# A hybrid attention, retention and mixture-of-experts block: new order and finer pieces at its head, its first refills and its tail

## The reference

```python
h = rms_norm(x, norm1_gain)
proj = h @ w_in          # attention q, k, v; indexer q, k, w; retention q, k, v, gate
out_a = dsa_attention(...)   # 64 of 256 keys chosen by the indexer, 8 heads
out_b = silu(g_b) * group_norm(retention(rotary(q_b), rotary(k_b), v_b))
x = x + concat(out_a, out_b) @ w_out
h2 = rms_norm(x, norm2_gain)
logits = h2 @ w_router + b_router          # 32 experts, top 4, softmax over the four
for e in range(32):
    z = h2 @ w1[e] + b1[e]                 # 1024 -> 2048, glu and lin interleaved
    act = glu * sigmoid(1.702 * glu) * (lin + 1)     # glu, lin clamped at 7
    out += combine[:, e] * (act @ w2[e] + b2[e])     # 1024 -> 1024
return rms_norm(x + out, final_gain)
```

## Time and profile before

| | |
|---|---|
| timed runs, median of 3 | 1089.05 us (1087.67 to 1089.17) |
| profiled execution, its own time | 1086.36 us |
| its span | 1084.6 us |
| TensorE matmul busy | 1038.4 us (96%) |
| VectorE, ScalarE busy | 302.7 us (28%), 157.0 us (14%) |
| mean granted TensorE clock | 0.985 |
| DMA, mean over the span | 396 GB/s, 429.75 MB |

### The profile page before, as it was taken

One profiled execution on the slowest core, in us unless ns is written; L12 is line 12 of the kernel. 1 busy time (PEld: TensorE's weight loads), 2 busy tenths in 40 slices (PEclk: granted clock), 3 DMA queues, 4 the chain that ended last, 5 costly groups with the idle time before them and its releaser, 6 DMA issues.

```text
span 1084.6 us, 11586 instructions
## 1 busy us (share of the span) xinstructions
PE 1038.4 (96%) x4616; PEld 397.4 (37%) x4616; DVE 302.7 (28%) x705; ACT 157.0 (14%) x281; POOL 22.2 (2%) x29
## 2 busy tenths in 40 slices
PE   9999999999999999899999999898989898999996
PEld 7458454333333333233332323232323232333332
DVE  2455623322222223122221312221223222221221
ACT  1231333110101111101010111011111101011111
POOL 1212000000000000000000000000000000000000
PEclk9999999999999999999998999999999999899999
DMA  9886946999999999999999999999999999999995
GB/s 328 238 252 264 387 161 242 429 431 432 432 426 431 433 430 429 431 433 429 429 431 433 428 430 432 425 432 430 431 433 431 433 431 428 430 433 431 424 428 208
DMA packets 34343, 429.75 MB, mean 396 GB/s; under 512 B 5036, under 2 KB 6480, under 8 KB 16496
## 3 DMA queue, kind: packets, MB, share of 16 engines
q1 hardware_dynamic: 32400, 426.03, 93.2%
q10 hardware_dynamic: 1216, 1.70, 1.1%
q0 software_dynamic: 704, 1.71, 0.6%
HBM read 426.80 MB, written 2.62 MB: 396 GB/s over the span
## 4 chain that ended last, share of the span: by engine, by line
PE 67%; DMA 31%; DVE 1%; SPq 1%; issue 0%; ACT 0%; DVEq 0%
PE ps L1326 28%; DMA w1r<-w_mlp 22%; PE ps L1352 13%; DMA w2r<-w_mlp 6%; PE ps L1393 5%; PE ps L1076 4%; PE ps L1304 3%; PE ps L1064 3%; DMA w1r<-w_out 1%; PE ps L1123 1%; PE ps L1229 1%; PE ps L1366 1%; PE ps L1198 1%; DMA w1r<-w_in 1%; PE ps L1334 1%; PE ps L1312 1%
## 5 line engine op out<-in xcount | busy, mean ns | idle before, releaser
L1326 PE MATMUL ps<-w1r,arena 128*64 128x512 f32 x2048 | 487.7, 612 | 28.0 <-DMA w1r<-w_mlp 27.2
L1326 PEld LDWEIGHTS ps<-w1r,arena 128*64 128x64 f32 x2048 | 139.2, 139 | 295.7 <-issue 257.5
L1352 PE MATMUL ps<-w2r,arena 128*64 128x512 f32 x960 | 211.8, 593 | 4.5 <-DMA w2r<-w_mlp 4.5
L1352 PEld LDWEIGHTS ps<-w2r,arena 128*64 128x64 f32 x960 | 68.7, 137 | 142.8 <-issue 135.3
L950 DVE TENSOR_TENSOR acc<-ps,acc 128x512 f32<-128x512 f32 x56 | 36.1, 686 | 180.5 <-PE ps L1393 180.5
L942 DVE TENSOR_TENSOR arena<-arena 128x512 f32<-128x512 f32 x32 | 22.2, 692 | 157.5 <-ACT arena L571 157.4
L575 ACT ACTIVATE arena<-ps 128x512 f32<-128x512 f32 x32 | 19.1, 597 | 289.0 <-PE ps L1334 289.0
L914 DVE TENSOR_TENSOR arena<-ps,cols 128x512 f32<-128x512 f32 x32 | 22.1, 692 | 137.6 <-PE ps L1312 135.9
L1304 PE MATMUL ps<-h,arena 128*64 128x512 f32 x248 | 58.5, 592 | 0.0
L1393 PE MATMUL ps<-arena 128*128 128x512 f32 x112 | 55.5, 618 | 0.0
L580 ACT ACTIVATE arena<-ps 64x512 f32<-64x512 f32 x29 | 17.1, 591 | 263.8 <-PE ps L1352 263.8
(11 more groups left out here) (252 smaller groups left out, 575.4 us busy)
## 6 DMA issues: line engine op xcount, KB each, us to landing
w1r<-w_mlp SPq DMA_DIRECT2D x54, 4096.0 KB, 32.0
w2r<-w_mlp SPq DMA_DIRECT2D x60, 2048.0 KB, 18.9
w1r<-w_mlp SPq DMA_DIRECT2D x22, 2048.0 KB, 10.6
w1r<-w_in SPq DMA_DIRECT2D x7, 2048.0 KB, 17.3
w1r<-w_out SPq DMA_DIRECT2D x2, 2048.0 KB, 13.7
w1r<-w_mlp SPq DMA_DIRECT2D x3, 1024.0 KB, 7.3
rel_table<-arena ACTq DMA_DIRECT2D x1, 1536.0 KB
acc<-x SPq DMA_DIRECT2D x2, 512.0 KB, 4.6
```

The costliest lines, as they stand in the source:

```text
L1326: ins = mm(ps[64 * c:64 * c + 64, 2 * par + n, :], hgT[:, par, k % 4, 64 * (k // 4):64 * (k // 4) + 64], w1r[:, 8 * par + k, at:at + 512], ...
L1352: ins = mm(ps[at:at + 64, 4 + c, :], actT[:, k % 4, 64 * (k // 4):64 * (k // 4) + 64], w2r[:, k // 2, col:col + 512], start=(k == 0), stop ...
```

## The change

It has seven parts.

1. `win[0]` is loaded in two halves of 1 MB, the first ahead of `wki`, the second behind it. The product of `C_QI` runs with k outside and the four groups inside, and waits for each half on its own.
2. The slot numbers are shifted by FAR, so that `rank` needs no subtraction.
3. In the route stage the `ones` product and `gather_first(0)` come directly behind `route(1)`, and `z_bias` comes behind the second rank product.
4. The first `hg` copy, its transposes (to banks 7 and 6) and the first `take_hgT` are split in two halves of 256 columns; rows 0 and 1 of expert 0 need the first half only.
5. In the first step of a sweep the gather of expert 1 stands behind row 3 and its transposes behind row 4. Rows 0 to 3 of expert 2 are refilled singly.
6. In `final` the transposes of expert 30's activation move ahead of rows 6 and 7 (to `actT_30`, in the space of `b2f`), `add_expert(0, 0, gT)` ahead of `down` of expert 29, `open_sum(1)` between the two halves of that `down`; `add_pair(0)` becomes two `add_expert`.
7. The result is stored in two pieces of 512 KB; `fg_in` and `stored` become one semaphore.

```diff
+        actT_30 = b2f[:, :].rearrange("p (c n) -> p c n", c=4)
...
-    slot = np.tile(np.arange(SLOTS, dtype=np.float32), (P, 1))
+    slot = np.tile(np.arange(SLOTS, dtype=np.float32) + FAR, (P, 1))
...
+            sp.dma_start(win[0][:, 0:4], win_v[:, 0:4, CHUNK_COL[0]:CHUNK_COL[0] + 512]).then_inc(win_half, 16)
             sp.dma_start(wki, win_v[:, :, 2048:2120]).then_inc(wki_in, 16)
-            load_win(0)
+            sp.dma_start(win[0][:, 4:8], win_v[:, 4:8, CHUNK_COL[0]:CHUNK_COL[0] + 512]).then_inc(win_in[0], 16)
...
-                sp.wait_ge(w1_used, 8 * base + 1)
-                sp.dma_start(w1r[:, 0, :], w1_v[2, 0, 0, :, 0:2048]).then_inc(w1_early, 16)
-                sp.wait_ge(w1_used, 8 * base + 2)
-                sp.dma_start(w1r[:, 1, :], w1_v[2, 0, 0, :, 2048:4096]).then_inc(w1_in[0], 16)
-                next_w1(base, 2, 0, range(1, 4))
+                for k in range(4):
+                    sp.wait_ge(w1_used, 8 * base + k + 1)
+                    sp.dma_start(w1r[:, k, :], w1_v[2, 0, k // 2, :, 2048 * (k % 2):2048 * (k % 2) + 2048]).then_inc((w1_early, w1_in[k // 2])[k % 2], 16)
+                next_w1(base, 2, 0, range(2, 4))
...
-            for i, (t, c) in enumerate(((0, 0), (0, 1), (1, 0))):
-                sp.wait_ge(res_ready, i + 1)
-                sp.dma_start(out_v[:, t, 512 * c:512 * c + 512], res[:, t, 512 * c:512 * c + 512]).then_inc(stored, 16)
+            sp.wait_ge(res_ready, 2)
+            sp.dma_start(out_v[:, 0], res[:, 0, :]).then_inc(last_dma, 16)
             sp.wait_ge(fin_root, 3)
-            sp.dma_start(out_v[:, 1, 512:1024], res[:, 1, 512:1024]).then_inc(stored, 16)
-            sp.wait_ge(stored, 64)
+            sp.wait_ge(res_ready, 3)
+            sp.dma_start(out_v[:, 1], res[:, 1, :]).then_inc(last_dma, 16)
+            sp.wait_ge(last_dma, 48)
...
-            nc.scalar.activation(hg, ps[:, 4, :], ACT.Copy).then_inc(first_copied, 1)
+            for i in range(2):
+                nc.scalar.activation(hg[:, 256 * i:256 * i + 256], ps[:, 4, 256 * i:256 * i + 256], ACT.Copy).then_inc(first_copied, 1)
...
                 sigmoid(base, NE - 2)
+                take_act(base, NE - 2, actT_30)
                 take_gT(hb, NE // 2 - 1, gT_last)
...
-                link(v.tensor_scalar(rank[:, t, :], rank[:, t, :], -FAR, None, ALU.add))
...
+            def take_first_hgT():
+                for i in range(2):
+                    dve.wait_ge((first_made, hg_tr)[i], 2 - i)
+                    ins = v.tensor_tensor(hgT[:, 0, 2 * i:2 * i + 2].rearrange("p j (c n) -> p (j c) n", c=2),
+                                          ps[:, 7 - i, 256 * i:256 * i + 256].rearrange("p (b n) -> p b n", b=4),
+                                          cols[:, GQ + 4 * i:GQ + 4 * i + 4].rearrange("p (b a) -> p b a", a=1).to_broadcast((P, 4, SLOTS)),
+                                          ALU.mult)
+                    ins.then_inc((hgT_part, hgT_sb)[i], 1)
...
-            chunk(C_QI, 2, by_head)
+            for k in range(KD):
+                if k % 4 == 0:
+                    pe.wait_ge((win_half, win_in[0])[k // 4], 16)
+                for g in range(4):
+                    ins = mm(ps[:, 2 + g // 2, S * (g % 2):S * (g % 2) + S], win[0][:, k, P * g:P * g + P], hT[:, k, :],
+                             start=(k == 0 and g % 2 == 0), stop=(k == KD - 1 and g % 2 == 1))
+            ins.then_inc(proj_done, 1)
...
-            pe.wait_ge(bias_part, 3)
-            pe.wait_ge(sel_first, 1)
-            z_bias(0, 0, 0, free=False)
+            mm(ps[:, 6, 64 + NE:64 + 2 * NE], ones, chosen[:, 0, :], start=True, stop=False)
             gather_first(0)
-            mm(ps[:, 6, 64 + NE:64 + 2 * NE], ones, chosen[:, 0, :], start=True, stop=False)
             pe.wait_ge(chosen_ready, 2)
             mm(ps[:, 6, 64 + NE:64 + 2 * NE], before, chosen[:, 1, :], start=False, stop=True).then_inc(rank_mm, 1)
+            pe.wait_ge(bias_part, 3)
+            pe.wait_ge(late_consts, 2)
+            z_bias(0, 0, 0, free=False)
             gather_first(1).then_inc(first_made, 1)
...
-            pe.wait_ge(first_copied, 1)
-            for j in range(4):
-                ins = nc.tensor.transpose(ps[:, 7, P * j:P * j + P], hg[:, P * j:P * j + P], ident)
-            ins.then_inc(hg_tr, 1)
+            for i in range(2):
+                pe.wait_ge(first_copied, i + 1)
+                for j in (2 * i, 2 * i + 1):
+                    ins = nc.tensor.transpose(ps[:, 7 - i, P * j:P * j + P], hg[:, P * j:P * j + P], ident)
+                ins.then_inc((first_made, hg_tr)[i], 1)
...
-                gather(base, e + 1, 1 - par)
+                if not head:
+                    gather(base, e + 1, 1 - par)
+                if head and isinstance(base, int):
+                    pe.wait_ge(hgT_sb, base + e + 1)
                 z_rows(base, lap, 2, par, halves)
                 if par == 1 and not first:
                     scatter(base, hb, m - 1, 0)
                 z_rows(base, lap, 3, par, halves)
-                gather_T(base, e + 1)
+                if head:
+                    gather(base, e + 1, 1 - par)
+                else:
+                    gather_T(base, e + 1)
                 z_rows(base, lap, 4, par, halves)
+                if head:
+                    gather_T(base, e + 1)
...
-                for k in range(4, 7):
+                for k in range(4, 6):
                     z_rows(base, lap, k, 1, False)
+                act_T(base, e - 1)
                 gates_T(base, hb, NE // 2 - 1)
-                z_rows(base, lap, 7, 1, False)
-                down(base, wb, e - 2, 1)
-                act_T(base, e - 1)
+                for k in range(6, 8):
+                    z_rows(base, lap, k, 1, False)
+                pe.wait_ge(based, 2 * rb + 1)
+                pe.wait_ge(y_sb, base + e - 2)
+                add_expert(0, 0, gT)
+                down(base, wb, e - 2, 1, ks=range(4))
                 pe.wait_ge(z_read, base + e + 1)
                 open_sum(1)
+                down(base, wb, e - 2, 1, ks=range(4, 8))
                 pe.wait_ge(actT_sb, base + e)
                 act_T(base, e, lin_last)
-                pe.wait_ge(based, 2 * rb + 1)
                 pe.wait_ge(y_sb, base + e - 1)
                 pe.wait_ge(y_dve, 3 * rb + 1)
-                add_pair(0)
+                add_expert(0, 1, gT)
                 pe.wait_ge(based, 2 * rb + 2)
                 add_pair(1)
-                down_late(0, 0, actT, range(8), {0: 0, 4: 1}, hb)
+                down_late(0, 0, actT_30, range(8), {0: 0, 4: 1}, hb)
```

More of the change, by code:

```diff
@@ L222, in hybrid_block @@
         p_ready = sem("p_ready"); gated_ready = sem("gated_ready"); gathered = sem("gathered")
-        hg_sb = sem("hg_sb"); hg_tr = sem("hg_tr"); hgT_sb = sem("hgT_sb")
+        hg_sb = sem("hg_sb"); hg_tr = sem("hg_tr"); hgT_sb = sem("hgT_sb"); hgT_part = sem("hgT_part")
         z_read = sem("z_read"); glu_ready = sem("glu_ready");
@@ L229, in hybrid_block @@
         y_dve = sem("y_dve"); part_sum = sem("part_sum"); based = sem("based"); fin_sq = sem("fin_sq"); fin_inv = sem("fin_inv"); fin_root = sem("fin_root"); res_ready = sem("res_ready")
-        fg_in = sem("fg_in"); stored = sem("stored")
+        last_dma = sem("last_dma")
         block = ctx.enter_context(nc.Block())
@@ L590, in take_gateT @@
             def take_gateT():
-                act.wait_ge(first_made, 2)
+                act.wait_ge(first_made, 3)
                 nc.scalar.activation(gateT[:, :], ps[:, 4, 0:P], ACT.Copy).then_inc(first_copied, 1)
@@ L615, in final @@
                 take_y_half(base, NE - 3, 1)
-                take_act(base, NE - 2)
                 take_act(base, NE - 1, actT_last)
@@ L752, in _ @@
                 ins = v.tensor_scalar(sel_z[:, e, :], pick[0:96, e:e + 1].to_broadcast((96, SLOTS)), 1.0, None, ALU.mult)
-            ins.then_inc(sel_first, 1)
+            ins.then_inc(late_consts, 1)
             for t in range(TT):
@@ L997, in sweep @@
                     gates()
-                    dve.wait_ge(gq_sb, 1)
+                    dve.wait_ge(late_consts, 1)
                 else:
                     one_hot(base, 0, 0, free=False)
-                take_hgT(base, 0, 0)
+                if start:
+                    take_first_hgT()
+                else:
+                    take_hgT(base, 0, 0)
                 step(base, hb, 0, 0, first=True)
@@ L1030, in result @@
                                        fgb[:, 512 * c:512 * c + 512], ALU.mult, ALU.mult).then_inc(res_ready, 1)
-            dve.wait_ge(fg_in, 16)
+            dve.wait_ge(last_dma, 16)
             dve.wait_ge(scattered, n * NE)
@@ L1338, in hgT_until, with down @@
                 return min(e + 3, NE) if isinstance(e, int) else e + 3
-            def down(base, wb, e, par, free=True):
+            def down(base, wb, e, par, free=True, ks=range(8)):
                 pe.wait_ge(actT_sb, base + e + 1)
@@ L1345, in down @@
```

(11 more changed lines are left out.)

9 lines of the change are left out of this document (5 added, 4 removed).

## The result

| | before | after |
|---|---|---|
| median of 20 runs each | 1087.53 us | 1090.95 us |
| lowest to highest | 1085.83 to 1089.52 | 1084.91 to 1095.67 |
| profiled execution, own time | 1086.36 | 1090.57 |
| its span, mean granted clock | 1084.6, 0.985 | 1088.8, 0.979 |

The ratio is 1.0028, with a 95% interval of 1.0016 to 1.0041: slower by about 3 us. The forecast was 1086.4, 0.24% faster, with a range up to 1089.0. The time is outside the range, on the other side of no change. The runs of after also spread over 10.8 us, where those of before spread over 3.7. In the batches timed later the kernel before was not always so narrow: 35 runs beside e1 to e4 lie between 1086.16 and 1095.16.

The account below looks back on a forecast made before the run. The sweep was taken as a weight stream at the DMA rate, with gains only in head, stream start and tail. Terms +1.1 - 1.3 - 0.7 - 1.25 - 0.5 = -2.65 from 1089.05 gave 1086.4 us, range 1084.2 to 1089.0.

Parts of the forecast that it names:

- the +1.1 for the first chunk in halves: Head: the first half delays `wki`, so the first chunk starts at 15.6 instead of 14.49; 1.1 us lost.
- B: Head: the clock falls in TensorE's new hole, stretching the matmuls behind it by 1.9 us; 1088.3, chance 0.22.
- E: Head: the clock falls and the thin `wki` product doesn't bring it back; +3.7 in all, 1092.8, chance 0.07.
- the sum of -2.65: Whole kernel: head +1.1, route -1.3, refills -0.7, tail -1.25 and stores -0.5 together, in us.
- Route, -1.3: Route stage: bias product moved 0.3, subtraction removed 0.2, `hg` in halves 0.8; first `z` row 1.3 us earlier.
- Refills, -0.7: Start of the sweep: later gather and four single refills keep the weight stream without a hole; 0.7 us gained.
- Tail, -1.25: Tail: work moved into TensorE's waits ahead of `w2[29]`'s second half starts the last `w1r` products earlier; 1.25 us gained.
- Stores, -0.5: End: two stores of 512 KB instead of four, the last landing at 1083.7 instead of 1084.2; 0.5 us gained.
- the bound of +0.3: Stores at the end: worst case of that step, since the first bytes leave 0.7 us later; 0.3 us lost.

Follow-up runs that it names:

- e1: Changed kernel with the load of `wki` moved ahead of both halves of `win[0]`: 1084.05 us beside 1087.61 for the kernel before, ratio 0.9967.
- e4: Changed kernel with `wki` loaded ahead of both halves and the result stored in four pieces of 256 KB: 1084.01 us beside 1087.61, ratio 0.9961.
- e2: Kernel before with only the first chunk's halves around `wki`, the new loop order and two merged semaphores: 1090.44 us beside 1087.61, ratio 1.0023.
- e3: Changed kernel with five products on zeros added ahead of TensorE's wait for `wki`: 1086.38 us beside 1087.61 for the kernel before, ratio 0.9984.
- f2: e4 with the gather of expert 1 and the refills of expert 2 as in the kernel before: 1084.95 us beside 1087.67, ratio 0.9967.
- g3: Changed kernel with one product on zeros (two matmul instructions) ahead of the wait for `wki`: 1090.71 us beside 1088.15 for the kernel before, ratio 1.0017.
- f3: e4 with the route stage of the kernel before (subtraction, bias product first, `hg` in one piece): 1085.12 us beside 1087.67, ratio 0.9977.
- g1: Kernel before with only the tail fillers of the change added: 1086.69 us beside 1088.58 for the kernel before, ratio 0.9989.
- f1: e4 with the tail order of the kernel before, no fillers: 1083.67 us (6 runs) beside 1087.67, ratio 0.9959.
- g2: The same kernel as f1, timed again: 1084.31 us (6 runs) beside 1088.58 for the kernel before, ratio 0.9963.
- f4: Kernel before with only its four stores of 256 KB replaced by two of 512 KB: 1088.28 us beside 1087.67, ratio 1.0003.

## Why the prediction was wrong

**The step that failed is the +1.1 for the first chunk in halves.** Its times are right: `wki` lands at 10.7 (10.9 foreseen), the product starts at 10.76 (11.0), and where the clock holds, the chunk starts at 15.3 (15.6; e2, e3). The Trainium skill ("DMA: Bandwidth & Descriptors", Queues, rings and completion order) has each engine take one ring's descriptors in order; the landing of `wki` behind the half agrees with it. But the sum charged the hole for its lateness only. What the hole does to the clock was put into rivals B and E, with 0.22 and 0.07, and 17 of 20 runs took that way: all from 1088.7 up have a mean granted clock of 0.975 to 0.980, the two shortest, 1084.91 and 1085.11, have 0.984, and one, at 1087.04, has 0.981. The mean doesn't say where in a run the clock fell: f2's profile has 0.980 with no fall in the head, and the kernel before has 0.980 or less in 10 of its 97 runs beside the experiments. So 17 is a count by an indirect sign; that the head is the place is shown by the traces of after and g3, and by e1 and e3, where no run of 24 is below 0.981.

The working for those chances was thin. The rows had an idle time of 1.99 without a cost and one of 2.47 with it, and the hole was foreseen at 2.2, so the trace of before had nothing for a chance of 3 in 10. "Before, the same product ran at the full clock" was no reason: before, it stood behind an idle time of 0.23. B's price of 1.9 is a slip too: by the earlier trace rows it is 5.35 - 3.65 = 1.7.

**The cost, by rows of after.** The next stage starts 5.77 later (34.36 instead of 28.59). Product start 10.76 - 8.96 = +1.80. The product +1.76. From its end to the chunk -0.27: the two table products take 0.61 more at the lower clock, but the wait of 0.88 for `win[0]` is gone. The chunk, 34.15 - 17.78 = 16.37 against 13.89 before, +2.48. Sum 5.77. The clock's part is 1.76 + 0.61 + 2.48 = 4.9, and e3 against the changed kernel gives 4.6 in the medians. Rival E asked for 3.76 + 2.6 = 6.4, from a product at half speed throughout; in the trace its first part still ran at 1.00. E's 1092.8 is only 1.8 above the median, but by luck: 1.5 of that is the base (next paragraph), and the 1.5 too much for the clock is nearly made up by stores and tail, which gave less than E assumed.

**The base.** The three runs of before had a median of 1089.05, the twenty have 1087.53. So the sum of -2.65 would have given 1084.9 from the better base, and the forecast was 1.5 milder than its own sum. The profile was nearer, with 1086.36.

**B or E?** E by its mechanism. The thin product didn't bring the clock back, nor did the first part of the chunk: 0.50 until 22. B would have been a loss of 1.9.

**Route, -1.3: right.** 8.17 became 6.97, -1.20 in the rows, and f3's row against e4's gives 1.19. One VectorE instruction stands between the rank product and the pick.

**Refills, -0.7: the step is right, its size is not pinned down.** The pair is issued 191.41 - 178.39 = 13.0 after the first row, as foreseen, and the hole in the DMA share is gone (0.61 to 0.99). That the two profiled executions give just -0.71 is partly luck: the same distance varies by up to 2.0 between profiles with the same refills, and their medians are 1.1 apart.

**Tail, -1.25: the step is right, what reaches the end depends on the kernel.** From the second half of `w2[29]` to the products it is 7.51, foreseen 7.4. g1 gives 1.2. In the profiled pair only 0.68 of it is left: from the stream's last wait to that second half it takes 1054.03 - 984.95 = 69.08 after and 1049.18 - 980.90 = 68.28 before. After, the wait at 984.95 was 3.22 and the 16 matmuls behind it took 5.35, 1.7 more than the 3.65 of before behind 1.99; TensorE then has no waits left for the fillers to fill. In e4 against f1 and g2 the fillers gave nothing in the medians. The fair comparison is of profiles with the same last wait of the stream, 3.2 us with 5.35 behind it: from that wait to the last scatter it is 93.5 in the three with fillers (after, e3, f3) and 94.2 in two without (e2, g2), so 0.7. The third without, f1, has 95.55. In e4 itself it is 94.7, as in e1 (94.6): there the second half of `w2[29]` still waits 0.70 for its load, 69.9 after that last wait of the stream, where it starts 69.1 after it in after. The traces don't say why that load is later, so how much the fillers give in the best version stays open.

**Stores, -0.5: wrong sign.** From the last root's VectorE row to the end of the span it is 8.3 after, 8.5 in e1 and 8.3 in f4, all with two stores; 7.5 before, 7.7 in e4 and 7.5 in f1, all with four. Over all thirteen profiles it is 8.2 to 8.5 in the five with two stores and 7.3 to 7.9 in the eight with four, 0.7 apart on average. The last store is issued 3.3 after that row, as I had it, but lands 4.6 after its issue (f4: 4.7) where I took 3.3. Windows of after, last 5 us (DMA share and GB/s last):

```profile
1083.00:1084.00 1.00, 0.00 (x0) 0.00 (x0) 0.68 (x1) 0.65 (x1) 0.00 (x0) 1.00 0.54 193
1084.00:1085.00 1.00, 0.00 (x0) 0.00 (x0) 0.00 (x0) 0.00 (x0) 0.00 (x0) 0.66 0.94 373
1085.00:1086.00 1.00, 0.00 (x0) 0.00 (x0) 0.00 (x0) 0.00 (x0) 0.00 (x0) 0.50 1.00 397
1086.00:1087.00 1.00, 0.00 (x0) 0.00 (x0) 0.00 (x0) 0.00 (x0) 0.00 (x0) 0.50 0.21 82
```

The first store is issued at 1082.72, 2.26 after that VectorE row; before it was 1078.69 - 1077.10 = 1.59. So the stream of results starts 0.67 later, for which only the bound of +0.3 was set aside. From then on the DMA engines are busy at shares of 0.94 and 1.00 for both stores, and the second stands behind the first. The forecast priced the last store by itself, not the bytes ahead of it. The medians can't see this: e1 and e4 are equal, and f4 against before is 0.03% with an interval of -0.07 to 0.14%. The 3.2 that I worked out as an estimate from the Trainium skill ("DMA: Bandwidth & Descriptors", Anatomy of one DMA) for this store is 1.4 short of the 4.6 measured; the section gives its figures for the path over GpSimd, where SP issues these stores, and the estimate has no term for the bytes of the store ahead. That store is not the whole of the 1.4: the first one, with no bytes ahead of it, landed 3.8 after its issue, already 0.6 above the estimate.

**The best version** is e4: the changed kernel with `wki` first in its queue and four stores, 0.39% below the kernel before, [0.27, 0.51]. By its own rows it is 3.0 ahead at the wait near 572 (568.89 against 571.89: head 1.07, route 1.20, refills 0.73); the medians give 3.6 in all, so 0.6 is left for tail and scatter of the measurement. Four stores instead of two are in it for their rows, not for its median.

## What to carry to other kernels

Before a load is put ahead of another one, look at which of them TensorE takes first; a half that lands early is worth nothing if the operand that gates the engine's next instruction now stands behind it. Price a new hole in TensorE twice, by its length and by what the work behind it costs at the lower clock, and when the hole's length lies between two idle times of the trace, one with and one without a fall, give the fall an even chance. Many small gains are best added only after the term that could outweigh them has been measured by itself. And when the runs of a kernel spread, look at their mean granted clocks beside the median: here they fell into 0.981 to 0.984 and 0.975 to 0.980, with medians some 5 to 6 us apart; the spread alone proves little, for the kernel before once spread over 9.0 us too.

## What the runs showed that I had not expected

- After the hole, the clock did not fall at once: it was 1.00 from 10 to 12 and 0.76 from 12 to 13, and then stayed at 0.50 for 9 us of unbroken work on TensorE (after).
- The same program takes one or the other path from run to run: two or three of 20 (after), six of 12 (e2) and two of 12 (g3) had no such fall by their mean clock. Two readings are open: the hole's length moves with the landing of `norm_gain` (6.65 to 7.28), or the chip looks at TensorE's activity at moments that lie differently in each run. The Trainium skill ("TensorE: Matmul & The Clock Gate", What's actually happening) states that the chip's watch on the engine runs freely and doesn't start with the kernel, which would be the second. No run here separates the two, but the length of an idle time doesn't sort the cases by itself. In g3 the 2.16 of the head was followed by a fall, while the sweep of e4 had a wait of the same 2.16, and that of g3 itself one of 2.28, with the full speed behind it. The kind of work behind the wait differs too (128x72 in the head), and none of the runs varies that alone:

```profile
627.35 3.65 PE L1347 MATMUL ps<-w1r,arena 128*64 128x512 f32 x16 [2.16 <-DMA w1r<-w_mlp]
...
636.22 3.65 PE L1348 MATMUL ps<-w1r,arena 128*64 128x512 f32 x16 [2.28 <-DMA w1r<-w_mlp]
```
- More work can be less time: ten matmul instructions on zeros, 2.32 us, saved 4.6 us.
- The clock also fell without a hole. In the profiled execution of f2 the first gather took 1.73 instead of the 1.08 of after, though TensorE had waited for no more than 0.2 in the 10 us ahead of it. Its window has the clock at 0.66, with TensorE busy for all of the 4.00 us:

```profile
168.00:172.00 4.00, 4.00 (x17) 1.66 (x15) 1.42 (x8) 2.55 (x9) 0.00 (x0) 0.66 0.49 209
```

What starts such a fall stays open.
